# The activation tile H starts 64 bytes further along its partition, at the offset of the split weights

## What is computed

```python
def reference(x, c, ..., mem_2, ...):
    x = first_block(x, c, w_ada, ..., peer_u, peer_v, final_g)
    return second_block(x, mem_2, ..., ffn_w_up_2, ..., final_norm_g_2)

def first_block(...):
    hn = modulate(rmsnorm(x, norm1_g[l]), shift1, scale1)
    proj = hn @ w_in[l]                      # nine projections of hn
    ya = dsa_attention(...); yb = stick_breaking_attention(...)
    merged = sigmoid(ga) * (ya @ w_proj_a[l]) + sigmoid(gb) * (yb @ w_proj_b[l])
    x = x + gate1[:, None, :] * (merged @ w_out[l])
    hn2 = modulate(rmsnorm(x, norm2_g[l]), shift2, scale2)
    f = peer_ffn(hn2, peer_wq[l], peer_sub_keys[l], peer_u[l], peer_v[l])
```

## Time and profile before

| what | value |
|---|---|
| median of 3 runs | 1406.82 us (1403.36 to 1411.68) |
| the profiled execution | 1403.13 us |
| its span in the profile | 1401.4 us |
| TensorE (PE) busy | 1362.2 us, 97% |
| weight loads (PEld) busy | 1263.9 us, 90% |
| VectorE, ScalarE, GpSimd busy | 76%, 60%, 25% |
| mean DMA rate | 191 GB/s |

### The profile page before, as it was taken

The page is one execution under the profiler, slowest core; times in us unless marked ns, Lnnn a source line. Parts: engine busy times, 40 slices in busy tenths (PEclk is TensorE's granted clock), DMA queues, the critical chain, the costliest instruction groups (busy, mean ns, idle before and its releaser), DMA issues.

```text
span 1401.4 us, 25301 instructions
## 1 busy us (share of the span) xinstructions
PE 1362.2 (97%) x10150; PEld 1263.9 (90%) x10150; DVE 1070.9 (76%) x1841; ACT 834.5 (60%) x1447; POOL 353.5 (25%) x224
## 2 busy tenths in 40 slices
PE   7999999999998999999999999999999999899997
PEld 5988989999998999999988888887889889799997
DVE  7788898668899888889576666677668577898862
ACT  3556784454554788787554444555556667776641
POOL 3216101234444000000223223352223221432200
PEclk9999999999999999999999999999999999999999
DMA  9859774556554544544565566656566535375630
GB/s 386 283 190 308 235 248 174 193 166 193 191 189 151 183 162 155 161 158 163 171 220 196 192 193 191 224 177 197 195 221 245 168 121 181 117 228 189 203 107 31
DMA packets 73719, 268.21 MB, mean 191 GB/s; under 512 B 8401, under 2 KB 9730, under 8 KB 72834
## 3 DMA queue, kind: packets, MB, share of 16 engines
q1 hardware_dynamic: 71280, 256.41, 55.3%
q10 hardware_dynamic: 1426, 7.56, 1.5%
q0 software_dynamic: 896, 2.62, 0.5%
HBM read 262.88 MB, written 3.67 MB: 190 GB/s over the span
## 4 chain that ended last, share of the span: by engine, by line
PE 78%; DVE 14%; ACT 4%; DMA 2%; issue 1%; POOL 1%; DVEq 0%; ACTq 0%; POOLq 0%
PE bank L623 77%; DVE split L1850 3%; DVE ada_acc L1885 2%; DVE PR L2300 1%; POOL H L2666 1%; DVE PR L2297 1%; DMA ringb<-in_w_ada 1%; ACT split L1314 1%; DVE PR L2305 1%; DMA far<-in_w_pa 0%; DMA ringb<-in_w_g 0%; ACT PB L1428 0%; DVE H L2387 0%; DVE rT L1936 0%; DMA vecs<-in_vecs 0%
## 5 line engine op out<-in xcount | busy, mean ns | idle before, releaser
L623 PE MATMUL bank<-H,split 128*128 128x256 f32 x5928 | 713.3, 280 | 12.1 <-DVE split L1850 6.7
L623 PEld LDWEIGHTS bank<-H,split 128*128 128x128 f32 x5928 | 691.9, 189 | 18.9 <-DVE split L1850 8.5
L1314 ACT CAST split<-ringb 128x1024 fp32r<-128x1024 f32 x350 | 365.9, 1047 | 265.6 <-PE bank L623 252.9
L623 PE MATMUL bank<-split,H 128*128 128x512 f32 (+1 forms) x1728 | 390.1, 387 | 1.6 <-ACT PB L1333 1.4
L623 PEld LDWEIGHTS bank<-split,H 128*128 128x128 f32 x1728 | 320.3, 188 | 69.2 <-DVE split L1850 1.9
L2639 POOL TENSOR_TENSOR split<-ringb,split 128x1024 fp32r<-128x1024 f32 x89 | 220.1, 2473 | 639.1 <-ACT split L1314 639.1
L1850 DVE TENSOR_TENSOR split<-ringb,split 128x1024 fp32r<-128x1024 f32 x261 | 325.1, 1249 | 62.6 <-ACT split L1314 62.4
L2387 DVE TENSOR_TENSOR H<-PR,H 128x256 fp32r<-128x256 f32 x128 | 135.0, 1056 | 105.5 <-ACT H L1653 105.5
L1850 DVE TENSOR_TENSOR split<-far,split 128x1024 fp32r<-128x1024 f32 x78 | 101.1, 1304 | 34.1 <-ACT split L1314 33.9
L1314 ACT CAST split<-far 128x1024 fp32r<-128x1024 f32 x89 | 92.9, 1048 | 54.7 <-PE bank L623 40.9
L2653 POOL TENSOR_TENSOR rT<-rT 128x256 f32<-128x256 f32 x25 | 26.7, 1067 | 176.2 <-ACT rT L1363 174.6
(11 more groups left out here) (297 smaller groups left out, 1236.1 us busy)
## 6 DMA issues: line engine op xcount, KB each, us to landing
ringb<-in_u SPq DMA_DIRECT2D x128, 512.0 KB, 3.7
ringb<-in_v SPq DMA_DIRECT2D x128, 512.0 KB, 4.3
ringb<-in_w_ada SPq DMA_DIRECT2D x28, 512.0 KB, 5.6
far<-in_w_up SPq DMA_DIRECT2D x26, 512.0 KB, 4.5
far<-in_w_ada SPq DMA_DIRECT2D x20, 512.0 KB, 5.4
ringb<-in_w_up SPq DMA_DIRECT2D x17, 512.0 KB, 4.8
ringb<-in_w_pq SPq DMA_DIRECT2D x16, 512.0 KB, 4.3
far<-in_w_dn SPq DMA_DIRECT2D x14, 512.0 KB, 4.0
```

Of the source, the lines that this page charges most:

```text
L623: return TE.matmul(o, l, r, start=start, stop=stop, skip_group_check=True)
L1314: S.copy(buf(m)[0], slots[P.slot[m]]).then_inc(hi_done, 1)
```

## The change

H is taken from word 16 of `H_all` on, in place of word 0: its first byte and with it each of its rows moves by 64 bytes, to the place that cf has. Nothing else differs: no tile moves, and every instruction, semaphore and transfer is the same one.

```diff
         H_all = sb("H", [128, 16 + 16 * T], F32R)
-        H = H_all[:, 0:16 * T].rearrange("p (z k t) -> p z k t", z=2, k=8)
+        H = H_all[:, 16:16 + 16 * T].rearrange("p (z k t) -> p z k t", z=2, k=8)
```

## The result

The changed kernel took 1426.56 us (median of 4 runs, 1425.67 to 1427.57) against 1409.25 us (1403.36 to 1417.72, 4 runs) of the kernel before: a ratio of 1.0114 with a 95% interval of 1.0081 to 1.0148, 1.1% slower. Its profiled execution took 1425.67 us with a span of 1423.9 us, 22.5 us more than that of before. The forecast was 1406.2 us and no change, with a range up to 1425: it was wrong, and so was the range, if by 1.6 us. The rival "118 everywhere" (36%, 1424.8 us) named the right side and nearly the right time.

A forecast was written before the change was run, and what follows sets the result against it. TensorE, busy 1362.2 of 1401.4 us, was taken as the bound, through the time from matmul to matmul. H stationary gave -0.6 us, all other terms 0: 1406.8 became 1406.2 us, with a range of 1397 to 1425.

The forecast's parts named there:

- 118 everywhere: Rival, 36%: equal starts put all or the long segments with H moving at 118 ns, +18.0 us, 1424.8 us.
- The writers of H: The 28 writers of H's first part and 28 of the rest: taken as 0, at most 0.6 us either way.
- The term for H stationary: 144 matmuls of 512 columns in w_vb, w_va, w2_mv and w_va's 12 apart become equal to v's: 0.6 us gained.
- H moving: The 5928 matmuls with H as moving operand: taken as 0, between 7.6 us gained and 18.6 us lost.
- the share of today: Some segments with H moving swap between 113 and 118 ns, direction unknown, shares unchanged: 0 us; this case had 30%.
- Both signs: What would prove it wrong: one pace in all segments with H moving, or a third beside 113.3 and 118.0 ns.
- a rival at 22%: "113 everywhere": the 118 pace comes only where the operands differ in remainder, so all segments reach 113; 1398.6 us.
- The upper bound: Worst case for H moving: all 3950 matmuls at 113 go to 118 ns, 18.6 us lost.
- The evidence from the gates: Segments after gates read from xT (128) run at 118, after rT (0) at 113, in each of 21 rounds.
- The rule: Skill page: TensorE waits for nobody, weight loads have an independent read port; the offset would not matter, sum 0 instead of -0.6.

The follow-up runs named there:

- e12: Changed kernel plus 960 unused matmuls before unit 20 of u, five distances by four widths; at distance 0, 120.0 ns for 256 columns, 226.8 for 512.
- e2: Kernel before with H moved to 128 and, by placing mod in front, split to 64 (the two starts exchanged): 1427.36 us.
- e6: Kernel before with H moved to 192, mod placed behind H_all, split and cf still at 128: 1417.36 us.
- e8: Kernel before with mod placed in front of xT, so that xT alone moves from 128 to 64: 1401.16 us.
- e11: Kernel before with H taken from word 4 of H_all (at 80), 48 bytes below split: 1425.4 us.
- e3: Kernel before with H taken from word 8 of H_all (at 96), 32 bytes below split: 1423.98 us.
- e9: The same kernel as e8, timed against the kernel before: 1405.55 us against 1407.81, ratio 0.998 (0.9959 to 1.0001).

## Why the prediction was wrong

**What held.** The bound was named rightly: the span moved with the pace of L623. The writers of H kept their durations (no median moved by more than the 9 ns of L1940, 477 to 486), and v stayed at 226.7 ns. The term for H stationary had the right sign: 0.6 us were forecast, 0.10 + 0.15 + 0.08 = 0.33 us (and about none for the 12 apart) were measured. In the trace each of these short stages has its first 4 to 9 distances between 225 and 236 ns before it settles at 226.7; I had taken v's settled pace for them.

**The step that failed** is "H moving", at "Which value? ... I take the share of today: 0". It supposed that a new distance has the two paces of the old one and that a start only draws between them. Equal starts have one pace of their own, 120.0 ns: the term put at 0 measured +28.3 us of busy time. Both signs that the prediction named against itself came, one pace in all segments with H moving and a third pace beside the two. The trace of before had no matmul of 256 columns at distance 0, and I took a value between two bounds where none of the rows was at that distance. The nearest row was at 512 columns, where equal starts are the best of all; e12 shows the order turned round at 256. I wrote that this row proves little for 256, and yet let it hold a rival at 22%.

**The upper bound** was too low. It took 118, the slower of the two paces known, for the worst: 3950 matmuls from 113.3 to 118.0 ns were 18.6 us (17.6 with 117.8). At 120.0 ns the same counts give 3950 x 6.7 + 1980 x 2.2 = 30.8 us; the group's busy time grew by 28.3. That the median moved by only 17.3 us has two reasons: 4.9 us came out of TensorE's waits, and the profiled execution of before was a short one, 6.1 us under the median of its four runs, the changed one only 0.9.

**The rival "118 everywhere"** had the side, the place and 1424.8 us, but a wrong pace; that its time came so near is luck, since its loss of 18.0 us was too small for the products and the two reasons above made up for it. Its reason, that the load of the next weights meets the moving operand, is supported in part: with equal starts and 256 columns the loads do take 192 ns. As a rule it fails, for at 512 columns equal starts are the best, and at +64 (e2, e6) the pace is 117.8 with loads of 188, so that a slower pace needs no longer load. The evidence from the gates was real (e8 moved those segments by moving xT), but it concerned which pace a segment takes at -64, not the pace at 0.

**The rule.** The offsets matter with TensorE nearly alone at work (e12). By the Trainium skill, page "SBUF — State Buffer", section "SBUF: two separate sides", TensorE never waits for another engine; no run here speaks against that. The second read port for weight loads that the table there calls independent is another matter: loads and stream are not independent in time in these traces, 113.3 to 120.0 ns by distance alone.

**What stays open.** Why a distance costs what it costs at a width. The table is a measurement, not an explanation. Nor is it known what chooses the pace at -64 and at +64 for segments outside the gates, and e11 and e3 leave open whether a start off a multiple of 64 bytes costs by itself.

**A better version.** Of the layouts tried, H 64 bytes below split and cf equal to split, which is that of before, has the shortest times; moving xT to 64 with it measured 0.998 of before (0.9959 to 1.0001), which is not clear of no change. Its median of 1405.55 us is 21 us under the changed kernel's.

## What to carry to other kernels

When a kernel is bound by back-to-back matmuls with a weight load each, divide a window by its count before anything else: a step from 113.3 to 120.0 ns is nearly invisible in busy shares (97% and 98%), and the change from two paces to this one was 1.1% of this kernel. Take the pace from a long window or from the starts themselves: over 16 us a count gave 118.0 for 117.8. The offsets of the two operands are worth a measurement for each width in use: here the same distance was the worst of five for 256 columns and the best for 512. And where the new state has no row at all in the trace, the share of today is no forecast; bound it and say so.

## What the runs showed that was not expected

A third pace of 120.0 ns with loads of 192 ns. The order of distances that turns round between 256 and 512 columns (120.0 against 113.3, and 226.8 against 233.3 ns). And two stable paces, 113.3 and 117.8 ns, for the same instructions at the same addresses, not fixed by the program: the 942 matmuls of w_up ran at one in e8 and at the other in e9.
